# Weaving the second block's first two halves into the first block at every stage boundary of a two-layer trunk

## The reference

```
layer 0 mixer: proj = h @ w_in (2048 x 6144); cut into q, k, v, g, xb, gate
   retention (8 heads of 128, chunks of 64): rotary on q and k, decayed scores, values, norm, * silu(g)
   RG-LRU (8 blocks of 128): conv of 4 taps over xb, two gates, scan, * gelu(gate)
   y = concat(ret_out, lru_out) @ w_out
layer 1 mixer: h @ w_qkv (2048 x 2560); 4 KV groups of 8 heads of 64, window 128 in chunks of 64,
   softmax with a sink per head; y = out @ w_out
MLP of both:   u = relu(h @ w_up); y = (u * u) @ w_down
```

## Time and profile before

| | us |
|---|---|
| median of 3 runs | 2042.18 |
| lowest, highest | 2042.11, 2042.24 |
| the profiled execution, its own time | 2042.25 |
| its span, first to last instruction | 2040.4 |
| PE busy in it | 2006.0 |
| DVE busy | 1422.7 |
| ACT busy | 1019.6 |

### The profile page before, as it was taken

One profiled execution on the slowest core, in us unless ns is written; L12 is line 12 of the kernel. 1 busy time (PEld: TensorE's weight loads), 2 busy tenths in 40 slices (PEclk: granted clock), 3 DMA queues, 4 the chain that ended last, 5 costly groups with the idle time before them and its releaser, 6 DMA issues.

```text
span 2040.4 us, 24588 instructions
## 1 busy us (share of the span) xinstructions
PE 2006.0 (98%) x9195; PEld 1655.3 (81%) x9195; DVE 1422.7 (70%) x1931; ACT 1019.6 (50%) x1343; POOL 43.3 (2%) x55
## 2 busy tenths in 40 slices
PE   8999999999999999999999999999999999999997
PEld 6888888878888888888887877878888888888876
DVE  5776678887567657756888677978548756855864
ACT  5566665555345435434555554555445434534543
POOL 1110110000000000000000000000000000000000
PEclk9999999999999999999999999999999999999999
DMA  8556546656656665556656544566656566566552
GB/s 292 171 169 210 175 156 208 198 171 206 194 180 204 198 192 189 201 186 194 197 173 199 165 133 156 181 193 192 200 188 195 193 191 196 182 204 193 186 192 97
DMA packets 191612, 382.49 MB, mean 187 GB/s; under 512 B 6184, under 2 KB 6448, under 8 KB 191408
## 3 DMA queue, kind: packets, MB, share of 16 engines
q1 hardware_dynamic: 190288, 377.58, 57.1%
q0 software_dynamic: 1216, 3.88, 0.5%
q10 hardware_dynamic: 32, 0.01, 0.0%
HBM read 379.34 MB, written 2.10 MB: 187 GB/s over the span
## 4 chain that ended last, share of the span: by engine, by line
PE 89%; DVE 6%; ACT 3%; issue 1%; DMA 0%; ACTq 0%; SPq 0%; DVEq 0%
PE acc L1040 29%; PE acc L1042 29%; PE acc L1041 29%; DVE w_lo L722 2%; DVE turn L908 2%; ACT w_hi L537 1%; PE bank L1051 1%; PE bank L1130 0%; DVE a_lo L734 0%; ACT L601 0%; PE bank L1140 0%; PE bank L1154 0%; ACT area L627 0%; DMA x<-in_x 0%; ACT L607 0%
## 5 line engine op out<-in xcount | busy, mean ns | idle before, releaser
L722 DVE TENSOR_TENSOR w_lo<-raw,w_hi 128x1024 fp32r<-128x1024 f32 x712 | 867.1, 1225 | 550.5 <-ACT w_hi L537 548.0
L537 ACT ACTIVATE w_hi<-raw 128x1024 fp32r<-128x1024 f32 x712 | 748.2, 1059 | 835.6 <-PE acc L1042 835.3
L1040 PE MATMUL acc<-w_hi,a_hi 128*128 128x512 f32 x1568 | 616.3, 393 | 5.0 <-DVE a_lo L734 4.7
L1042 PE MATMUL acc<-w_hi,a_lo 128*128 128x512 f32 x1568 | 611.2, 390 | 0.0
L1041 PE MATMUL acc<-w_lo,a_hi 128*128 128x512 f32 x1568 | 611.0, 390 | 0.0
L1040 PE MATMUL acc<-w_hi,b_hi 128*128 128x512 f32 x1280 | 499.0, 390 | 4.9 <-DVE b_lo L730 2.6
L1042 PE MATMUL acc<-w_hi,b_lo 128*128 128x512 f32 x1280 | 498.0, 389 | 0.0
L1041 PE MATMUL acc<-w_lo,b_hi 128*128 128x512 f32 x1280 | 498.0, 389 | 0.0
L1040 PEld LDWEIGHTS acc<-w_hi,a_hi 128*128 128x128 f32 x1568 | 295.0, 188 | 68.8 <-DVE a_lo L734 6.0
L1042 PEld LDWEIGHTS acc<-w_hi,a_lo 128*128 128x128 f32 x1568 | 294.8, 188 | 61.9
L1041 PEld LDWEIGHTS acc<-w_lo,a_hi 128*128 128x128 f32 x1568 | 295.0, 188 | 60.1
(11 more groups left out here) (152 smaller groups left out, 522.6 us busy)
## 6 DMA issues: line engine op xcount, KB each, us to landing
raw<-in_mlp_w_up SPq DMA_DIRECT2D x128, 1024.0 KB, 5.6
raw<-in_mlp_w_down SPq DMA_DIRECT2D x128, 1024.0 KB, 5.1
raw<-in_hyb_w_in SPq DMA_DIRECT2D x48, 1024.0 KB, 5.1
raw<-in_attn_w_qkv SPq DMA_DIRECT2D x20, 1024.0 KB, 5.1
raw<-in_hyb_w_out SPq DMA_DIRECT2D x16, 1024.0 KB, 5.3
raw<-in_attn_w_out SPq DMA_DIRECT2D x16, 1024.0 KB, 5.1
x<-in_x SPq DMA_DIRECT2D x4, 512.0 KB, 9.7
out_y<-x SPq DMA_DIRECT2D x4, 512.0 KB, 4.0
```

What stands on the lines that cost most here:

```text
L537: nc.scalar.activation(w_hi[:, h % RING], raw[:, h // 2, 2 * (h % 2):2 * (h % 2) + 2, :], ACT.Copy).then_inc(hi_ready, 1)
L722: nc.vector.tensor_tensor(w_lo[:, h % RING], raw[:, h // 2, 2 * (h % 2):2 * (h % 2) + 2, :], w_hi[:, h % RING].bitcast(F32), ALU.subtract) ...
L1040: nc.tensor.matmul(a, xh, wh, start=first, stop=False)
L1042: ins = nc.tensor.matmul(a, xl, wh, start=False, stop=last)
```

## The change

It replaces `DOWN0` by `WOVEN`, all nineteen starts of a stage or of an MLP part, and orders two slots as halves 0 to 5 of the first block, 0 and 1 of the second, 6 and 7 of the first, 2 to 7 of the second. The wait on the turned output now stands at position 8 (tick 0 of the second slot), and a new wait before position 6 says that the accumulator of the block before is free. All that follows the first block of a pair (`post` on all engines) moves two ticks later (`late`). `q` and `k` are turned by PE after half 4 instead of 3 and copied out in tick 5. The last steps of attention group 3 come in the same ticks as the others'. The LRU waits of MIX_OUT0 are spread over three halves, and SP's loads take the block of the new order.

```
@@ -93,39 +93,46 @@
-TURN_AT = {"aq": 0, "q": 3, "k": 3, "g": 4, "xb": 2, "gate": 2, "kv": 2}
+TURN_AT = {"aq": 0, "q": 4, "k": 4, "g": 4, "xb": 2, "gate": 2, "kv": 2}
 QUADRANTS_AT = {"up": {1: 4, 2: 6, 3: 6}, "res": {1: 4, 2: 6, 3: 6}}
 STATIONARY_STARTS = ({MIX_OUT0, MLP0, QKV0, ATT_OUT0, MLP1}
                      | {m + PERIOD * c + COLS for m in (MLP0, MLP1) for c in range(CHUNKS)})
-DOWN0 = {m + PERIOD * c + COLS for m in (MLP0, MLP1) for c in range(CHUNKS - 1)}
-WOVEN = ([(0, k) for k in range(6)] + [(1, k) for k in range(6)]
-         + [(0, 6), (0, 7), (1, 6), (1, 7)])
+WOVEN = ({MIX_OUT0, QKV0, ATT_OUT0}
+         | {m + COLS * n for m in (MLP0, MLP1) for n in range(2 * CHUNKS)})
+WOVEN_ORDER = ([(0, k) for k in range(6)] + [(1, 0), (1, 1), (0, 6), (0, 7)]
+               + [(1, k) for k in range(2, 8)])
 def piece(b, k):
     for first in (b, b - 1):
-        if first in DOWN0:
-            d, h = WOVEN[HALVES * (b - first) + k]
+        if first in WOVEN:
+            d, h = WOVEN_ORDER[HALVES * (b - first) + k]
             return first + d, h
     return b, k
+def late(b):
+    return 2 if b in WOVEN else 0
 LRU_IN_SLOT = {2: 0, 3: 1, 4: 2, 5: 3, 8: 4, 9: 5, 10: 6, 11: 7}
+LRU_BEFORE = {2: 4, 4: 6, 5: 8}
 def lru_steps(b, k):
     return [(LRU_IN_SLOT[b - d], d * HALVES + k) for d in (1, 0) if b - d in LRU_IN_SLOT]
-def att_late(g):
-    return int(g < KV - 1)
+ATT_LATE = 1
@@ -143,9 +150,9 @@
-def out_at(kind):
-    return (max(QUADRANTS_AT[kind]) if kind in BY_QUADRANT else TURN_AT[kind]) + 1
+def out_at(kind, b):
+    return (max(QUADRANTS_AT[kind]) if kind in BY_QUADRANT else TURN_AT[kind]) + 1 + late(b)
@@ -436,22 +443,23 @@
-                        load(Slot(first + j, c), lambda g, d: up[c * COLS + j, g])
+                        load(Slot(first + j, c), lambda g, d: up[c * COLS + j + d, g])
...
-                load(Slot(QKV0 + n), lambda g, d: w_qkv[c, g])
+            qkv = [KV] + list(range(KV))
+            for n in range(len(qkv)):
+                load(Slot(QKV0 + n), lambda g, d: w_qkv[qkv[n + d], g])
@@ -562,7 +570,7 @@
-                act.wait_ge(half_used, slot.halves(0))
+                act.wait_ge(half_used, slot.halves(late(b)))
@@ -627,7 +635,7 @@
-                for tt in range(TT) if k == 6 + att_late(g) else ():
+                for tt in range(TT) if k == 6 + ATT_LATE else ():
@@ -638,12 +646,12 @@
-                if k == 0 and kind in BY_ACT:
+                if k == late(b) and kind in BY_ACT:
                     leave(slot, kind, j)
-                if k == 1 and kind in ("res", "fin"):
+                if k == 1 + late(b) and kind in ("res", "fin"):
                     act.wait_ge(evac_dve, slot.count(N_EVAC_DVE, 0))
                     square_sums(next_norm(b), j)
-                if kind in SPLIT and k == out_at(kind):
+                if kind in SPLIT and k == out_at(kind, b):
@@ -878,11 +886,11 @@
-                for tt in range(TT) if k == 4 + att_late(g) else ():
+                for tt in range(TT) if k == 4 + ATT_LATE else ():
-                for tt in range(TT) if k == 6 + att_late(g) else ():
+                for tt in range(TT) if k == 6 + ATT_LATE else ():
@@ -892,9 +900,12 @@
-                at = QUADRANTS_AT[kind]
+                at = {tick + late(slot.b - 1): n for tick, n in QUADRANTS_AT[kind].items()}
                 if k not in at:
                     return
+                if k == min(at):
+                    dve.wait_ge(turned_out, slot.count(N_TURNED, -1, INIT_HALVES))
@@ -921,13 +932,12 @@
-                late = 6 if b in DOWN0 else 0
-                if k == late and kind in ("res", "down", "fin"):
-                    dve.wait_ge(half_used, slot.halves(late))
+                if k == late(b) and kind in ("res", "down", "fin"):
+                    dve.wait_ge(half_used, slot.halves(late(b)))
                     for tt in range(TT):
                         xs = x[:, tt, j * NB:(j + 1) * NB]
                         nc.vector.tensor_tensor(xs, xs, acc[:, b % 2, tt, :], ALU.add).then_inc(evac_dve, 1)
-                if k == 1:
+                if k == 1 + late(b):
@@ -948,7 +958,7 @@
-                if kind in TURNED and k == out_at(kind):
+                if kind in TURNED and k == out_at(kind, b):
@@ -959,7 +969,7 @@
-                if k == 3 and kind == "fin" and j < COLS - 1:
+                if k == 3 + late(b) and kind == "fin" and j < COLS - 1:
@@ -1157,10 +1167,9 @@
-                late = att_late(g)
-                                 4 + late: [(att_turn, 0), (att_turn, 1)],
-                                 5 + late: [(att_value, 0), (att_value, 1)]}.get(k, []):
+                                 4 + ATT_LATE: [(att_turn, 0), (att_turn, 1)],
+                                 5 + ATT_LATE: [(att_value, 0), (att_value, 1)]}.get(k, []):
@@ -1188,17 +1197,19 @@
-                    if b == MIX_OUT0 and k in (2, 5):
-                        pe.wait_ge(lru_lo, LRU_BLOCKS - 1 + k // 5)
+                    if b == MIX_OUT0 and k in LRU_BEFORE:
+                        pe.wait_ge(lru_lo, LRU_BEFORE[k])
                     if b == ATT_OUT0 and k == 0:
                         pe.wait_ge(att_lo, TT * (KV - 1))
-                    if b == ATT_OUT0 and k == HALVES - 2:
+                    if b - 1 == ATT_OUT0 and k == 0:
                         pe.wait_ge(att_lo, TT * KV)
-                    if b in STATIONARY_STARTS - DOWN0 and k == HALVES - 2:
-                        pe.wait_ge(turned_out, slot.count(N_TURNED, 0, INIT_HALVES))
-                    if b in DOWN0 and k == HALVES - 2:
-                        pe.wait_ge(evac_act, slot.count(N_EVAC_ACT, 0))
-                    if b - 1 in DOWN0 and k == HALVES - 4:
+                    if b in WOVEN and k == HALVES - 2:
+                        if BLOCKS[b - 1][0] in BY_ACT:
+                            pe.wait_ge(evac_act, slot.count(N_EVAC_ACT, 0))
+                        else:
+                            pe.wait_ge(evac_dve, slot.count(N_EVAC_DVE, 0))
+                    if b - 1 in STATIONARY_STARTS and k == 0:
@@ -1215,7 +1226,7 @@
-                        if k == TURN_AT.get(kind):
+                        if kind in TURN_AT and k == TURN_AT[kind] + late(b - 1):
```

More of the change, by code:

```diff
@@ L430, in _ @@
             for j in range(COLS):
-                load(Slot(MIX_OUT0 + j), lambda g, d: w_out[j, g])
+                load(Slot(MIX_OUT0 + j), lambda g, d: w_out[j + d, g])
             def load_mlp(layer, first):
@@ L443, in load_mlp @@
                 for j in range(COLS):
-                    load(Slot(first + PERIOD * c + j), lambda g, d: up[c * COLS + j, g])
+                    load(Slot(first + PERIOD * c + j), lambda g, d: up[c * COLS + j + d, g])
                 for j in range(COLS):
-                    load(Slot(first + PERIOD * c + COLS + j), lambda g, d: down[c, j, g])
+                    load(Slot(first + PERIOD * c + COLS + j), lambda g, d: down[c, j + d, g])
             load_mlp(0, MLP0)
             w_qkv = units(t["attn_w_qkv"][0])
-            for n, c in enumerate([KV] + list(range(KV))):
-                load(Slot(QKV0 + n), lambda g, d: w_qkv[c, g])
+            qkv = [KV] + list(range(KV))
+            for n in range(len(qkv)):
+                load(Slot(QKV0 + n), lambda g, d: w_qkv[qkv[n + d], g])
             w_att = units(t["attn_w_out"][0])
             for j in range(COLS):
-                load(Slot(ATT_OUT0 + j), lambda g, d: w_att[j, g])
+                load(Slot(ATT_OUT0 + j), lambda g, d: w_att[j + d, g])
             load_mlp(1, MLP1)
```

## The result

The changed kernel takes 2028.16 us (median of 6 runs, 2027.72 to 2028.79); the kernel before took 2042.14 in the same runs (6 runs, 2040.97 to 2042.36). The ratio is 0.9933, 95% interval 0.9920 to 0.9946: 14.0 us off. The profiled execution took 2028.0 us by its own time, at a mean clock of 0.997.

The account below looks back on a forecast made before the run. The prediction took PE, busy 98% of the span, as the bound, so only stalls could change. Its terms, 9.5 + 1.8 + 1.4 + 1.4 = 14.1 us off, gave 2028.1 us, range 2026.4 to 2033.5.

Parts of the forecast that it names:

- Term A: Six boundaries (MIX_OUT0, QKV0, MLP0, MLP1, each MLP's last group): PE's waits for the turned block before half 6 go, 9.5 us.
- Term B: ATT_OUT0: the wait for the last head group's att_lo before half 6 moves to position 8 and goes, 1.8 us.
- Term C: Last attention group's turn: one half later, its sixteen transposes no longer split by a wait for the probabilities, 1.4 us.
- Term D: q and k turned one half later in four slots: rotation waits go, partly becoming waits on the LRU's convolution, 1.4 us.
- At nothing: Later post-processing, accumulator and turned_out waits, MIX_OUT0's LRU waits, already woven starts, SP's loads: no effect on the time.
- The narrow place: Slot after a woven start, eleven pairs: work 0.87 us later, half 7's weight split slack 2.5 to 1.6 us, no stall.
- (1): Term D pays in full because DVE's convolution comes early enough: 15.5 us off, 2026.7 us; chance 0.10.
- (2): Partial new waits for weights in the slot after or att_lo: gives back 5.5 us, about 2033 us; chance 0.12.
- (3): Accumulator bank switching costs: 2.9 us by restarts, 2031 us, chance 0.01; or 71 us at half clock, 2099 us, chance 0.01.
- (4): Half 7's weight split in the slot after becomes the bound: 2050 us, chance 0.05; milder, no change, chance 0.04.
- (5): The change weaves starts that never stalled: already in the sum, at nothing for twelve of nineteen; no chance given.

Follow-up runs that it names:

- e3: Changed kernel with four of nineteen starts (MIX_OUT0, QKV0, last group of each MLP) in plain order again; median 2033.99 us, ratio 0.9964.
- e10: Changed kernel with all eight up starts in plain order, the other eleven starts still woven; median 2031.18 us, ratio 0.9949.
- e5: Changed kernel with ATT_OUT0 in plain order and the last steps of attention group 3 one half earlier; median 2031.42 us, ratio 0.9949.
- e4: Changed kernel, all starts woven, with the last steps of attention group 3 one half earlier; median 2029.61 us, ratio 0.9942.
- e1: Changed kernel with q and k turned after half 3 again, weaving kept; median 2028.42 us, ratio 0.9936.
- e2: Kernel before with q and k turned after half 4, nothing woven anew; median 2040.71 us, ratio 0.9995.
- e7: Changed kernel with six extra DVE operations in the slot two after each of eleven up or res starts; median 2038.62 us, ratio 0.9986.
- e9: Changed kernel with DVE's convolution for LRU blocks 1, 2, 5, 6 in tick 1, ahead of one weight split; median 2025.49 us, ratio 0.9921.
- e8: Kernel before with six extra DVE operations in the slot two after each of eleven up or res starts; median 2044.61 us, ratio 1.0015.

## Why the prediction was right, point by point

The forecast was 2028.1 us within 2026.4 to 2033.5, and the median is 2028.16.

- **Term A**, 9.5, came out at 9.7 by the events of the two traces, and e3 and e10 together give 5.95 + 3.72 = 9.67. The six stalls and the matmul behind each sum to 9.5 in the trace before, as forecast; the other 0.2 lies in small steps of the matmuls that follow, which the forecast had not counted. The slacks that carried it were real: `a_lo` was forecast to end 18.0 us into MLP0's slot, and it does (start of the slot 393.89, end of the last row here 411.89):

```profile
410.22 1.67 DVE L742 SCALAR_TENSOR_TENSOR a_lo<-turn,vecs,a_hi 128x256 fp32r<-128x256 f32 x4
...
413.03 1.23 DVE L730 TENSOR_TENSOR w_lo<-raw,w_hi 128x1024 fp32r<-128x1024 f32 x1 [1.14 <-ACT w_hi L545]
```

  The second of these rows is the weight cut for position 8. It ends at 414.26, 20.4 into the slot, and is due at 21.76, as forecast.
- **Term B**, 1.8, is 1.81 by the traces and by e5 less e4. The sum behind it was a little off: 1.7 with the overlap of 0.16 makes 1.9. The idle before that product is 1.73 in the trace, and only 0.08 more came off; the matmuls ahead of it are value products, and their records overlap less. **Term C**, 1.4, is 1.41 by the traces and 1.40 by e4.
- **Term D**, 1.4, is the one that was mis-sized: 0.82 by the traces, 0.72 and 0.81 by e1 and e2. The mechanism was the one forecast, half of the wait turning into a wait on `area`. The step that failed is "the gates start at about 99.82 instead of 100.16. The gain is 0.34". The start is right in kind, but I charged term A with the slow restart behind a wait and left it out here, where a wait is added: the gates that used to be ready now issue in 0.53 us instead of 0.43. That makes 0.34 - 0.10 = 0.24 a slot, 0.96 in all. At the first product behind the gates of the four slots the two traces show gains of 0.23, 0.21, 0.24 and 0.23, together 0.91; another 0.08 is lost between these slots, at places that don't turn q or k, and its cause was not looked for.
- **The agreement of the total is in part luck.** The terms overstate the change by 14.1 - 13.75 = 0.35 us (D too large by 0.6, A too small by 0.2), and the start-up happened to be 0.41 shorter in the profiled execution after. The timed medians, with 14.0 off, can't tell 13.75 from 14.1.
- **At nothing.** The post-processing two halves later, the wait for the free accumulator and the one on `turned_out` left no row in PE's waits. The 590 us window without a stall is as long as before.
- **The narrow place**: shift 0.87 forecast, 0.76 to 0.77 found; slack 1.6 forecast, 1.78 found by e7. Above it the price is as said, 11 slots' worth of each microsecond.
- **Rivals.** (1) D in full: refuted by e1, e2 and the four waits on `area`; e9 shows what it would have taken. (2) Partial new waits: there is none. The one wait by `w_lo`, 0.2 us, is the start-up's and stands in the trace before too. (3) Bank switching: the window holds 2605 matmuls in 590.00 us at clock 1.00 with the up starts woven too, and e10, with eight starts fewer woven, is longer by its two stalls and by nothing else. That stretch doesn't bear out the Trainium skill's warning (TensorE: Matmul & The Clock Gate, A second HAM failure mode: psum-queue depth-cycling); PE has no idle between the groups here, which is what the page's kernel had. (4) The weight cut of half 7 as the bound: refuted, and e7 shows that the place was the right one to fear, since six small operations in each of eleven slots give back 10.8 of the 14 us. (5) Weaving starts that never stalled: confirmed at nothing for the six up starts by e10. For the `down` starts that were woven before, it rests on the window alone.

## What to carry over

Where one engine is busy 98% of the time and its records are evenly spaced, a reordering is priced stall by stall: idle, plus the part of it that the modelled end hides, plus the slower issue behind every wait, with the opposite sign for every wait that the change adds. Count each operand's end from the start of its slot and compare it with the new due time; slacks worked out in this way held to 0.1 to 0.2 us, and a dose of dummy work measures them where the records leave doubt. Where a new wait is left, look first at what stands ahead of its releaser in the in-order queue: moving the convolution ahead of one weight cut (e9) gave 2.3 us, more than turning q and k later.

## What I had not expected of the hardware

- The restart behind a wait cost the same 0.10 to 0.11 us whatever the length of the wait: where 0.17 us was lost (e8), after 0.31 us of idle (gates, 0.53 for 0.43), after 0.79 (e7, 0.34 for 0.227) and after the 1.58 of the earlier trace rows. It isn't peculiar to waits: behind attention matmuls, without idle, the second product also starts 0.11 late (before, at 1153.75), and behind transposes 0.09 (at 97.31).
- A stall can be missing from the waits. In e8 PE lost 0.17 us at each of eight places, and the waits show none of them; their only row for `w_lo`, below, is the start-up's at 12.61. A matmul's record lasts 0.39 us by its modelled end while its successor may start after 0.227, so up to 0.16 us of a stall lies under the record. The distance from start to start shows it.

```profile
PE acc L1054 <- DVE w_lo L729: 0.3, 1, 0.3
```

- The start-up, up to the first turn through PE, differs by 1.3 us between the thirteen profiled executions (45.60 to 46.93) with the same instructions. The first product starts at 12.28 to 13.18; behind it two (e2) to nine (before, e5, e8) distances are of 0.40 us or more instead of 0.227, and from the first product to the first turn it takes 32.90 to 34.32 accordingly. In every trace the record of the granted clock begins, with full clock, within 0.25 us of where the pace changes (16.63 before, 15.65 after); for the slow products ahead of it there is no record. An effect of under 1 us can't be read from the span of one profile.
